# Two more pairs of MLP panels as seven block products, woven with the last whole panels

## The reference, cut to what matters

```python
x = x + mixed @ w_out                                   # "out", 8 panels
h = rmsnorm(x, norm_mlp)
x = x + jnp.square(jax.nn.relu(h @ w_ff1)) @ w_ff2      # w_ff1: 1024 x 4096, w_ff2: 4096 x 1024
return rmsnorm(x, norm_final)
```

## Time and profile before

| | |
|---|---|
| median of 3 runs | 777.65 us |
| profiled execution | 777.13 us |
| its span | 775.3 us |
| PE busy | 764.9 us (99%) |
| DVE busy | 498.7 us (64%) |
| ACT busy | 393.4 us (51%) |
| POOL busy | 279.6 us (36%) |

### The profile page before, as it was taken

How to read it: one execution, slowest core, us unless ns; L and a number is a source line. 1 busy time by engine, 2 the same in 40 slices (tenths; PEclk the granted TensorE clock), 3 DMA queues, 4 the chain that set the end, 5 groups by cost and what they waited for, 6 DMA issues and landing times.

```text
span 775.3 us, 11284 instructions
## 1 busy us (share of the span) xinstructions
PE 764.9 (99%) x3956; PEld 632.2 (82%) x3956; DVE 498.7 (64%) x1025; ACT 393.4 (51%) x734; POOL 279.6 (36%) x366
## 2 busy tenths in 40 slices
PE   8999999999999999999999999999999999999996
PEld 6878888888877787778888888888888888888895
DVE  7546557787757676635444747787777777876334
ACT  6433324688966566565245654444444444443321
POOL 1255424511113332146556553333333322233630
PEclk9999999999999999999999999999999999999999
DMA  7963013210150111134332324322223333332213
GB/s 263 342 202 144 1 57 106 83 55 28 32 160 29 55 42 41 41 108 152 108 108 82 109 82 135 109 90 96 89 87 102 109 109 109 109 109 82 92 45 109
DMA packets 26003, 77.77 MB, mean 100 GB/s; under 512 B 3710, under 2 KB 6966, under 8 KB 25695
## 3 DMA queue, kind: packets, MB, share of 16 engines
q1 hardware_dynamic: 23868, 74.72, 29.4%
q10 hardware_dynamic: 2083, 2.37, 1.0%
HBM read 73.90 MB, written 2.13 MB: 98 GB/s over the span
## 4 chain that ended last, share of the span: by engine, by line
PE 92%; DVE 4%; ACT 2%; issue 1%; DMA 1%; POOL 0%; DVEq 0%; SPq 0%
PE bank L1568 31%; PE bank L1979 20%; PE bank L1951 10%; PE bank L1953 5%; PE bank L1885 2%; PE bank L1867 2%; PE bank L1799 2%; PE bank L1919 2%; PE bank L1923 2%; PE bank L1924 2%; PE bank L1844 1%; PE bank L1817 1%; PE bank L1580 1%; PE bank L1581 1%; PE bank L1582 1%; PE bank L1699 1%
## 5 line engine op out<-in xcount | busy, mean ns | idle before, releaser
L652 POOL TENSOR_TENSOR wlo<-wraw,whi 128x256 fp32r<-128x256 f32 x344 | 265.1, 803 | 455.4 <-ACT whi L693 372.7
L693 ACT ACTIVATE whi<-wraw 128x1024 fp32r<-128x1024 f32 x77 | 80.7, 1054 | 27.7 <-PE bank L1979 16.0
L1568 PE MATMUL bank<-hh,wlo 128*128 128x512 f32 x304 | 81.0, 396 | 0.7 <-DVE gm L1231 0.5
L1568 PE MATMUL bank<-hl,whi 128*128 128x512 f32 x304 | 80.6, 392 | 0.0
L1568 PE MATMUL bank<-hh,whi 128*128 128x512 f32 x304 | 79.6, 391 | 0.0
L1568 PEld LDWEIGHTS bank<-hh,whi 128*128 128x128 f32 x304 | 56.6, 188 | 11.7
L1568 PEld LDWEIGHTS bank<-hl,whi 128*128 128x128 f32 x304 | 56.4, 188 | 11.7 <-issue 0.2
L1568 PEld LDWEIGHTS bank<-hh,wlo 128*128 128x128 f32 x304 | 55.4, 188 | 12.8 <-DVE gm L1231 0.9
L1979 PE MATMUL bank<-r_l,whi 128*128 128x512 f32 x224 | 57.9, 390 | 0.0
L1979 PE MATMUL bank<-r_h,wlo 128*128 128x512 f32 x224 | 56.3, 392 | 0.0
L1979 PE MATMUL bank<-r_h,whi 128*128 128x512 f32 x224 | 55.7, 389 | 0.0
(11 more groups left out here) (316 smaller groups left out, 1611.6 us busy)
## 6 DMA issues: line engine op xcount, KB each, us to landing
wraw<-in_panels SPq DMA_DIRECT2D x101, 512.0 KB, 3.3
land<-in_panels SPq DMA_DIRECT2D x12, 512.0 KB, 4.5
w1k<-in_w SPq DMA_DIRECT2D x1, 2048.0 KB, 9.8
w1v<-in_w SPq DMA_DIRECT2D x1, 2048.0 KB, 15.0
svraw<-in_panels SPq DMA_DIRECT2D x4, 512.0 KB, 5.0
hank<-bias_by_distance SPq DMA_DIRECT2D x4, 512.0 KB, 6.4
x_res<-in_xT SPq DMA_DIRECT2D x4, 512.0 KB, 4.5
out_dram<-x_res SPq DMA_DIRECT2D x12, 128.0 KB, 1.8
```

The lines of the kernel that those rows point to most:

```text
L652: ins = nc.gpsimd.tensor_tensor(wlo[:, s, k:k + 2], wraw[s][:, k:k + 2], whi[:, s, k:k + 2].bitcast(F32), ALU.subtract)
L693: A(whi[:, s], wraw[s][:], ACT.Copy).then_inc(w_hi, 1)
L1568: ins = M(b[:, cols], lhs, (xl if a == 1 else xh)[:, row + k, cols], start=(m == 0), stop=(m == 23))
```

## The change

The last four whole panels of the first quarter (4 to 7) become pairs 0 and 1; the twelve pairs of before become pairs 2 to 13. Whole panels 2 and 3 stay. The first two rounds have no panels of the second matrix between their products; the three first pairs and the whole panel 3 are interleaved by a written-out list on each engine. Pair 0 and 1 use slots 0 and 1, all others slots 2 and 3 as before; panels 2 and 3 move to slots 2 and 3, and to PSUM banks 4 and 5. There are buffers of their own for the sums of pairs 1 and 2, a second landing buffer and a second `tmp` for odd pairs.

```diff
+    if p < P_FF + 2:
+        return p % RING          # slot of a panel
     if p < P_FF2:
-        return p % RING
+        return 2 + p % 2
...
@@ SP
-            panel_loop(P_UP + 2 * RING, P_FF2)
+            panel_loop(P_UP + 2 * RING, P_FF + 2)
+            def late_panel(p, used):
+                sp.wait_ge(w_used, used + 1)
...
+            pair_second(0)
+            sp.wait_ge(w_used, P_OUT + 6 + 1)
+            pair_first(0)
+            late_panel(P_FF + 2, P_FF)
+            sp.wait_ge(pd_lo, 1)
+            pair_second(1)
+            late_panel(P_FF + 3, P_FF + 1)
+            pair_second(2)
+            sp.wait_ge(w_used, P_FF + 2 + 1)
+            pair_first(2)
+            result(sp, ("wx", 0))
+            pair_first(1)
+            result(sp, ("wx", 1))
+            late_panel(P_FF2, P_FF + 3)
+            result(sp, ("wx", 2))
+            pair_first(3)
+            sp.wait_ge(pd_lo, 2)
+            pair_second(3)
+            result(sp, ("wr", 1))
+            late_panel(P_FF2 + 1, P_FF + 3)
...
@@ ACT
             for n in range(KT):
...
-                split(P_OUT + n + RING)
+                if n < 6:
+                    split(P_OUT + n + RING)
+                if n == 6:
+                    pair_first_high(0)
+                    for i in range(4):
+                        sum_high(0, i)
...
             for i in range(4):
+                if i == 2:
+                    split(P_FF + 2)
                 act.wait_ge(hx_raw, i + 1)
                 A(th[:, i], tr[:, i], ACT.Copy).then_inc(hx_hi, 1)
+            pair_second_high(0)
...
+            split(P_FF + 3)
+            plain_high(0)
+            plain_high(1)
+            pair_first_high(2)
+            plain_high(2)
+            m2_high(0)
+            for i in range(4):
+                sum_high(2, i)
+            plain_high(3)
+            m7_high(0)
+            pair_first_high(1)
+            u2_high(0)
...
+            second_tile_high(1)
+            pair_first_high(3)
+            u2_high(2)
+            split(P_FF2 + 1)
...
@@ DVE
+                if n == 6:
+                    first_sums(0)
+                    third_sum(0)
+                    fourth_sum(0)
+                    pair_first_low(0, 0)
+                    pair_first_low(0, 1)
+                    sum_low(0, S3)
...
+            pair_second_low(0)
+            sum_low(0, S2)
             dve.wait_ge(rs2, 1)
...
+            for n in range(2):
+                plain_positive(n)
+                hidden_low(n)
+            plain_positive(2)
+            sum_low(0, S1)
+            hidden_low(2)
+            c11(0)
+            first_sums(2)
+            third_sum(2)
+            fourth_sum(2)
+            sum_low(0, S4)
+            plain_positive(3)
+            hidden_low(3)
+            m7_low(0)
+            first_sums(1)
+            third_sum(1)
+            fourth_sum(1)
+            u2(0)
+            pair_first_low(1, 0)
+            pair_first_low(1, 1)
+            c22(0)
+            sum_low(1, S3)
+            c21(0)
+            pair_first_low(2, 0)
+            c12(0)
+            sum_low(1, S2)
+            c11(1)
+            m7_low(1)
+            hidden_low(4)
+            hidden_low(5)
+            pair_first_low(2, 1)
+            sum_low(1, S1)
+            u2(1)
...
@@ PE
-            for n in range(2, 8):
-                panel(P_FF + n, ("ff", 0, n), h2h, h2l)
+            panel(P_FF + 2, ("ff", 0, 2), h2h, h2l)
...
+            m1(0)
+            m2(0)
+            pe_.wait_ge(hx_lo, 4)
+            m7(0)
+            panel(P_FF + 3, ("ff", 0, 3), h2h, h2l, 0, 12)
+            m6(0)
+            panel(P_FF + 3, ("ff", 0, 3), h2h, h2l, 12, 24)
+            m5(0)
+            m1(1)
+            m4(0)
+            m3(0)
+            m2(1)
+            m7(1)
+            m1(2)
+            m6(1)
+            m2(2)
+            m5(1)
+            m4(1)
+            m3(1)
+            m7(2)
+            m6(2)
+            second_product(0, last_rows_last())
+            m5(2)
+            second_product(1, by_weight())
+            m4(2)
+            m3(2)
+            for j in range(3, N_SEVEN):
+                m1(j)
+                m2(j)
+                m7(j)
+                second_product(2 * j - 4, by_weight())
+                m6(j)
+                second_product(2 * j - 3, by_weight(), 0, 12)
+                m5(j)
+                second_product(2 * j - 3, by_weight(), 12, 24)
+                m4(j)
+                m3(j)
```

More of the change, by code:

```diff
@@ L176, in source, with pair_source, pair_slot, landings @@
     m = p - P_FF2
-    return P_FF2 + 4 * (m // 2) + 2 + m % 2 if m < 2 * N_SEVEN else P_FF2 + 2 * N_SEVEN + m
+    return P_FF + 8 + 4 * (m // 2) + 2 + m % 2 if m < 24 else P_FF + 32 + m
+def pair_source(j, o):
+    return P_FF + 4 + 2 * j + o if j < 2 else P_FF + 4 * j + o
+def pair_slot(j):
+    return 0 if j < 2 else 2
+def landings():
+    count = [13 * 16] * RING
+    got = {}
+    def land(name, s):
+        count[s] += 16
+        got[name] = count[s]
+    land(("pair", 0), 0)
+    land(P_FF + 2, 2)
+    land(P_FF + 3, 3)
+    land(("pair", 1), 0)
+    land(("pair", 2), 2)
+    for m in range(32):
+        if m % 2 == 0 and m < 22:
+            land(("pair", 3 + m // 2), 2)
+        land(P_FF2 + m, slot(P_FF2 + m))
+    return got
+LANDED = landings()
 def in_slot_ahead_of(p):
+    if p < P_FF + 2:
+        return panel_product(p - RING)
     if p < P_FF2:
-        return panel_product(p - RING)
+        return "ff", 0, p - P_FF - 2
     m = p - P_FF2
     if m < 2:
-        return "ff", 0, 6 + m
+        return (("wx", 1), ("wr", 1))[m]
     if m < 24:
@@ L618, in _, with pair_first, pair_second @@
[L618 to L621, removed]
+            def pair_first(j):
+                s = pair_slot(j)
+                sp.dma_start(wraw[s][:], panels[pair_source(j, 0)].rearrange("p (k m) -> p k m", k=8)).then_inc(w_in[s], 16)
+            def pair_second(j):
+                sp.dma_start(second_raw(j)[:], panels[pair_source(j, 1)].rearrange("p (k m) -> p k m", k=8)).then_inc(land2_in if j == 2 else land_in, 16)
@@ L919, in pair_second_high, with plain_high @@
[L919 to L930, removed]
+            def plain_high(n):
@@ L931, in _, with first_tile_high @@
                 stored(act, ("ff", 0, n))
                 hidden_high(n)
[L933 to L939, removed]
-            def c12_high(j):
[L941 to L947, removed]
-                pair_second_high(j)
[L949 to L957, removed]
+            def first_tile_high(j):
+                act.wait_ge(pos1, j + 1)
+                hidden_high(4 + 2 * j)
@@ new lines, in _ @@
+            m2_high(0)
[5 more added lines that the diff above has]
+            u2_high(0)
+            for i in range(4):
+                sum_high(1, i)
+            pair_second_high(1)
+            pair_second_high(2)
+            c12_high(0)
+            m2_high(1)
+            first_tile_high(0)
+            m7_high(1)
+            second_tile_high(0)
+            u2_high(1)
+            split(P_FF2)
@@ L958, in _ @@
                 if j + 1 < N_SEVEN:
                     pair_first_high(j + 1)
-                act.wait_ge(u2_ready, j + 1)
-                A(u2s[:], bank[j % 2][:, 0:T // 2], ACT.Copy).then_inc(u2_copied, 1)
-                split(P_FF2 + 2 * j + 2)
+                u2_high(j)
+                split(P_FF2 + 2 * j - 2)
                 if j + 1 < N_SEVEN:
@@ L1379, in add_product @@
                 emptied(V.tensor_tensor(x_res[:, n], ps[:], x_res[:, n], ALU.add), name)
[L1381 to L1412, removed]
[L1413 to L1419 removed]
             def c11(j):
[L1423 removed]
+                a, x, t = bank[j % 2], bank[2], joined(j)[:, 0, near]
                 dve.wait_ge(x_copied, j + 1)
@@ L1444, in c22 @@
             def c22(j):
-                a, t = bank[j % 2], tmp[:, 1, far]
+                a, t = bank[j % 2], joined(j)[:, 1, far]
                 dve.wait_ge(v_ready, j + 1)
@@ L1469, in c21, with plain_positive @@
                 dve.wait_ge(c22_made, 3 * j + 3)
-                positive(tmp[:, 1], tmp[:, 1], ALL_T).then_inc(pos2, 1)
-            for n in range(8):
+                positive(joined(j)[:, 1], joined(j)[:, 1], ALL_T).then_inc(pos2, 1)
+            def plain_positive(n):
                 ps = result(dve, ("ff", 0, n))
@@ L2094 @@
     parts.append(ff1[0:8])
-    for j in range(N_SEVEN):
-        q, i = divmod(j, 4)
-        parts += [ff1[8 + 2 * j:10 + 2 * j], ff2[q][2 * i:2 * i + 2]]
+    for m in range(0, 24, 2):
+        q, i = divmod(m, 8)
+        parts += [ff1[8 + m:10 + m], ff2[q][i:i + 2]]
     parts.append(ff2[QF - 1])
```

261 lines of the change are left out of this document (180 added, 81 removed).

## The result

The changed kernel takes 797.97 us (median of 5 runs, 797.22 to 799.4) against 777.65 us: ratio 1.0267, 95% interval 1.0254 to 1.028. The prediction was 796.5, range 788 to 802. The profiled execution took 797.64 us with a span of 795.8.

What follows compares the result with a forecast made beforehand. PE was taken as the bound without a gap. New waits and slow matmuls of 21.3 us, less 2.2 us of saved matmuls, add 19.1 us to 777.13, giving 796.2 and a median forecast of 796.5 us, range 788 to 802.

Steps and rivals of the forecast that it cites:

- What bounds the kernel: PE bounds the kernel without a gap, with 92% of the chain; every wait newly laid on it is lost in full.
- Whole panel 2: PE waits from 440.62 to 447.35 for POOL's low part of the panel loaded into slot 2: 6.7 us, bounds 6.3 to 7.3.
- The clock: PE's clock falls to half after each of the two long waits: 1.7 us booked twice, ends nothing to 3.4 us each.
- M6 and M5 of pair 0: PE waits 1.35 us at M6 for c11 behind panel 3's load, and 6.7 us at M5 for u2(0) behind DVE's row.
- The small waits: DVE a step late at M2 and M6 of pair 2, ACT and POOL at second-matrix panel 1: 3.1 us, 0 to 6.
- In the loop no cost: M4 and M3 change places in the loop; c12 comes 1.4 us later, M7's bank is free 0.4 us early: no cost.
- (a): Rival: the weave works and PE is never short, -2.2 us, 775.4 us; chance 0.04.
- (b): Rival: only the load of panel 2 costs and the later waits vanish, 783.9 up to 788 us; chance 0.09.
- (c): Rival: four loads land late, clock stays low after 473, small waits add up: +2 to +6 us, 799 to 803; chance 0.13.

Runs made afterwards that it cites:

- e1b_load23: Changed kernel with whole panel 3 loaded right behind panel 2, and panel 2 loaded early into the second landing buffer: 795.66 us, ratio 1.0237 to the kernel before.
- e9_early2: e7_all with whole panel 2 loaded early into the second landing buffer and ACT's split of second-matrix panel 1 moved ahead of pair 1's tiles: 783.8 us, ratio 1.0082.
- e4_clock: Changed kernel with unused filler matmuls, 33 ahead of whole panel 2 and 28 ahead of M5 of pair 0, keeping PE busy: 796.58 us, ratio 1.0249.
- e1_load3: Changed kernel with whole panel 3 loaded right behind whole panel 2, ahead of SP's wait for pd_lo 1: 797.7 us, ratio 1.0270.
- e6_order: Changed kernel with u2(0), pair 1's four sums and its first low part moved ahead of whole tile 3 on DVE and ACT: 792.91 us, ratio 1.0205.
- e5_highfirst: e1_load3 with whole panels 2 and 3 multiplying their high weights first (15 matmuls needing only ACT's copy), low weights after: 794.01 us, ratio 1.0218.
- e7_all: e5_highfirst and e6_order together, plus second tmp for pair 0, c11(0) right behind tile 1, pair 2's sums behind tile 3: 787.23 us, ratio 1.0129.
- e3_u2: Changed kernel with only u2(0) and its ACT copy moved ahead of whole tile 3: 799.96 us, ratio 1.0291.
- e8_pool: e7_all with the eight low parts of the sums of pairs 1 and 2 made by POOL in place of DVE: 788.44 us, ratio 1.0145.
- e10_both: e8_pool and e9_early2 together: 784.38 us, ratio 1.0097.

## Why the prediction was right

**What bounds the kernel.** That PE had no slack was the step on which all else stood, and it held: of the 20.8 us that the weave grew, all arrived at the end of the span.

**Whole panel 2.** Right in place and cause; mis-sized by 1.2 us, and at 7.9 above the term's own bound of 7.3. (Its lower bound was 6.3, but four instructions of 2.83 us in place of 3.50 make it 6.0.) The term that failed is POOL's four instructions, booked at 3.50 us from before and measured at 4.74; "nothing of this depends on whose panel it is" was wrong for them. In the kernel before, DVE's four low parts of the activation sums (439.58 to 444.2) were nearly through when POOL began; after, ACT's third copy stands behind that of panel 2, and so DVE's last two low parts start 1 us after POOL starts. The trace of before has a row for this that the prediction didn't use, the panel between the two of the earlier trace rows, beside DVE's activation sums:

```profile
433.10 5.47 POOL L652 TENSOR_TENSOR wlo<-wraw,whi 128x256 fp32r<-128x256 f32 x4 [2.62 <-ACT whi L693]
```

The cost of a moved instruction depends on what runs beside it where it lands. e1b_load23 and e9_early2 show the same at 5.7 and 5.8 us.

**The clock.** Both long waits were followed by matmuls at half speed, 1.5 and 2.05 us for the 1.7 booked twice, and e4_clock shows the first to be absorbed by M6's wait. What a wait costs in clock varies: e1_load3 lost 1.2 us more than the changed kernel in the same place. The granted clock of the stretch from 473 to 482 us is 0.69, a mixture of 1.2 and 2.4 GHz, and PE had done nothing for 6.56 us of the time before. In e6_order, where its waits are 1.6 and 1.7 us, the block products behind them run at full speed. The length of the wait alone doesn't decide it: the first 15 matmuls of panel 2 lost 1.7 us behind a wait of 2.83 us in e5_highfirst and nothing behind 2.89 us in e7_all, at the same place (PE's timelines, in this order):

```profile
443.69 5.25 PE L2148 MATMUL bank<-h,whi 128*128 128x512 f32 x15 [2.83 <-ACT whi L763]
444.18 3.69 PE L2148 MATMUL bank<-h,whi 128*128 128x512 f32 x15 [2.89 <-ACT whi L763]
```

**M6 and M5 of pair 0.** 1.2 us for 1.35 and 6.7 for 6.7. M5's row was read instruction by instruction, and it holds: DVE's `positive` started at 467.84, `hidden_low` 1.91 later, `u2` at 473.89 (DVE's timeline after).

```profile
467.84 0.69 DVE L1548 SCALAR_TENSOR_TENSOR tmp<-bank,rstd_b 128x512 f32<-128x512 f32 x1 [0.84 <-PE bank L1760]
469.75 0.69 DVE L1558 TENSOR_TENSOR r_l<-tmp,r_h 128x512 fp32r<-128x512 f32 x1 [1.22 <-ACT tmp L1012]
...
473.89 0.41 DVE L1586 TENSOR_TENSOR u2s<-bank,u2s 128x256 f32<-128x256 f32 x1
```

e3_u2 and e6_order confirm that the row, not `u2`, is the cause.

**The small waits.** 3.3 us for 3.1, in part by luck: the places named took 0.8 (M2 of pair 2), 0.6 (M6 of pair 2) and 1.0 us (second-matrix panel 1), 2.4 together, and 0.7 came at two not named, M3 of pair 1 and M7 of pair 2. "In the loop no cost" held: from pair 3 on PE doesn't wait until the last 10 us.

**The rivals.** (a), that PE is never short, fell with the first wait. (b), that only the first load costs, is contradicted by e5_highfirst: with that wait down to 2.8 us the kernel is still 17 us above the one before. (c) named lateness in the right place but in the wrong engine: something came late, but POOL's low part and not the DMA; panel 3's load took 4.3 us for the 4.5 booked (449.07 to 453.39). Its slow stretch after 473 us cost 2.05 us for 1.7.

## What to carry to other kernels

A saving of matmuls is worth its time only where the other engines can feed the denser schedule: here 2.2 us of PE were bought with two more pairs at 14.5 us of DVE's work each, in a stretch where PE gives DVE only 9.8 us a pair, and with the rearrangements of e9_early2 the kernel was still 6 us slower. When a wait stands in a long in-order list, find the whole row in front of it before moving one instruction; moving one hands the wait to the next consumer of that row. Start a freshly loaded operand with the part that is ready first: reordering the matmuls of two panels took 4.9 us out of a wait and 4.0 off the time, by the ratio, with the loads as they were (e5_highfirst against e1_load3).

## What the runs showed of the hardware that was not expected

POOL's and DVE's instructions slow each other when both read two tensors from SBUF: POOL's four 128x256 subtractions took 2.83, 3.50, 4.74, 5.47 and 5.74 us with 0, 1.1, 3.8, 5.2 and 5.5 us of such DVE instructions beside them (before at 427.66 and 443.84, after, before at 433.10, e1b_load23), so they grew by 0.5 to 0.6 us for each us of overlap; DVE's 128x512 ones took 1.22 us for 0.68. DVE's 128x256 instructions with a PSUM source kept their 0.42 us. Moving work from DVE to POOL gained nothing (e8_pool, e10_both). What half speed costs behind a wait differs from kernel to kernel: 1.5 us in the changed kernel and 2.7 in e1_load3 behind the same wait, 1.3 to 1.7 us behind waits of 2.44 (e4_clock, e8_pool, e10_both) and 2.83 us (e5_highfirst), and nothing behind 2.89 and 3.09 us (e7_all, e8_pool, at panel 2).
